# One GpSimd instruction of 1024 columns for each low part of a weight slot

## The reference

```
for layer in range(2):  x = x + mix(rmsnorm(x) @ w_in) @ w_out     # mLSTM, gated linear attention, sparse attention
h = h + 0.5 * swiglu(rmsnorm(h))                                   # FFN 1, inner width 2816
h = h + (gate_a * (attention @ w_a) + gate_g * (gmlp @ w_g)) @ w_out
h = h + 0.5 * swiglu(rmsnorm(h))                                   # FFN 2, inner width 2816
return rmsnorm(h)
```

## Time and profile before

| what | value |
|---|---|
| runs | 1190.82, 1191.22, 1198.76 us |
| profiled execution | 1191.43 us, span in the trace 1189.3 us |
| TensorE (PE) | 1151.8 us busy, 97% |
| VectorE (DVE) | 827.2 us busy, 70%, 1302 instructions |
| ScalarE (ACT) | 652.1 us, 55% |
| GpSimd (POOL) | 735.0 us, 62%, 552 instructions |
| mean granted TensorE clock | 0.991 |
| instructions in the span | 22346 |

### The profile page before, as it was taken

How to read it: one execution, slowest core, us unless ns; L and a number is a source line. 1 busy time by engine, 2 the same in 40 slices (tenths; PEclk the granted TensorE clock), 3 DMA queues, 4 the chain that set the end, 5 groups by cost and what they waited for, 6 DMA issues and landing times.

```text
span 1189.3 us, 22346 instructions
## 1 busy us (share of the span) xinstructions
PE 1151.8 (97%) x8970; PEld 1080.6 (91%) x8970; DVE 827.2 (70%) x1302; ACT 652.1 (55%) x1082; POOL 735.0 (62%) x552
## 2 busy tenths in 40 slices
PE   8979999999997999999999999999999999999996
PEld 6768998999986889899999999999789999999996
DVE  5877777669577876775876666666657667666664
ACT  7655773466575568435746444446566446444443
POOL 5668696567584768945675556566644664645552
PEclk9989999999998999999999999999999999999999
DMA  8443344546543433545466555554534554565550
GB/s 304 161 138 137 125 160 155 171 142 210 181 160 124 150 126 125 184 145 180 139 225 202 201 196 195 195 187 151 206 130 137 182 180 160 177 205 181 183 178 36
DMA packets 64118, 199.84 MB, mean 168 GB/s; under 512 B 6608, under 2 KB 17936, under 8 KB 64016
## 3 DMA queue, kind: packets, MB, share of 16 engines
q1 hardware_dynamic: 60048, 193.74, 47.8%
q10 hardware_dynamic: 3968, 4.69, 1.2%
HBM read 196.57 MB, written 1.84 MB: 167 GB/s over the span
## 4 chain that ended last, share of the span: by engine, by line
PE 85%; DVE 9%; ACT 3%; issue 2%; DMA 1%; ACTq 0%; DVEq 0%
PE ps L1582 47%; PE ps L1633 19%; PE ps L1623 9%; PE ps L1783 2%; DVE xs L930 1%; PE ps L1876 1%; DVE score L1073 1%; PE ps L1592 1%; ACT ring L438 1%; PE ps L1886 1%; DVE gb L1090 1%; DMA par<-in_par 1%; PE ps L1818 1%; PE ps L1857 0%; DVE ring L920 0%
## 5 line engine op out<-in xcount | busy, mean ns | idle before, releaser
L328 POOL TENSOR_TENSOR ring<-raw,ring 128x512 fp32r<-128x512 f32 x498 | 704.2, 1440 | 431.1 <-ACT ring L438 430.5
L1582 PE MATMUL ps<-xs,ring 128*128 128x256 f32 x5040 | 608.5, 281 | 1.9 <-DVE ring L920 1.6
L1582 PEld LDWEIGHTS ps<-xs,ring 128*128 128x128 f32 x5040 | 592.4, 190 | 9.6 <-issue 7.9
L438 ACT ACTIVATE ring<-raw 128x1024 fp32r<-128x1024 f32 x364 | 377.0, 1051 | 111.4 <-PE ps L1633 50.5
L920 DVE TENSOR_TENSOR ring<-raw,ring 128x1024 fp32r<-128x1024 f32 x115 | 162.1, 1411 | 121.9 <-ACT ring L438 121.7
L1633 PE MATMUL ps<-ys,ring 128*128 128x256 f32 x2016 | 241.7, 279 | 1.6 <-DVE ys L982 1.2
L1633 PEld LDWEIGHTS ps<-ys,ring 128*128 128x128 f32 x2016 | 237.2, 189 | 2.5 <-issue 2.5
L1623 PE MATMUL ps<-ring,xs 128*128 128x512 f32 x672 | 165.0, 398 | 0.0
L1623 PEld LDWEIGHTS ps<-ring,xs 128*128 128x128 f32 x672 | 123.0, 188 | 29.0 <-issue 3.6
L757 ACT ACTIVATE ys<-ca 128x256 fp32r<-128x256 f32 x44 | 18.3, 417 | 105.6 <-DVE ca L1377 105.6
L752 ACT ACTIVATE ex<-ex 128x256 f32<-128x256 f32 x44 | 18.2, 418 | 80.8 <-DVE ex L1363 80.8
(11 more groups left out here) (267 smaller groups left out, 1042.2 us busy)
## 6 DMA issues: line engine op xcount, KB each, us to landing
raw<-in_w SPq DMA_DIRECT2D x364, 512.0 KB, 3.5
y<-bias_rows ACTq DMA_DIRECT2D x6, 256.0 KB, 4.5
out_y<-y SPq DMA_DIRECT2D x4, 256.0 KB, 2.5
const<-in_const SPq DMA_DIRECT2D x1, 896.0 KB, 10.5
x<-in_x SPq DMA_DIRECT2D x3, 256.0 KB, 6.6
bias_rows<-lg ACTq DMA_DIRECT2D x1, 768.0 KB, 7.6
dec<-in_wT ACTq DMA_DIRECT2D x1, 512.0 KB, 3.5
qke<-in_ln ACTq DMA_DIRECT2D x1, 512.0 KB, 4.4
```

The lines of the kernel that those rows point to most:

```text
L328: last = pool.tensor_tensor(ring[:, g % RING, 1, half], raw[:, g % RAW, half], ring[:, g % RING, 0, half].bitcast(F32), ALU.subtract)
L438: act.activation(ring[:, g % RING, 0, :], raw[:, g % RAW, :], ACT.Copy).then_inc(S["hi"], 1)
L1582: last = mm(ps[bank][:, half * T:(half + 1) * T], ring[:, slot % RING, wp, (at + k) * P:(at + k + 1) * P], rhs(k, xp), start=(i == 0), sto ...
```

## The change

For each of its 249 slots GpSimd issues one subtraction over all 1024 columns, where it issued two over 512 columns each. The semaphore `lo` is raised by that one instruction; before, it was raised by the second of the two. Nothing else differs.

```
--- before.py
+++ after.py
@@ -323,11 +323,8 @@
                 g = p + RING
                 if not on_vector(p):
                     pool.wait_ge(S["hi"], reg * per + (g + 1))
-                    for a in range(0, SLOT, SLOT // 2):
-                        half = slice(a, a + SLOT // 2)
-                        last = pool.tensor_tensor(ring[:, g % RING, 1, half], raw[:, g % RAW, half],
-                                                  ring[:, g % RING, 0, half].bitcast(F32), ALU.subtract)
-                    last.then_inc(lo[g % RAW], 1)
+                    pool.tensor_tensor(ring[:, g % RING, 1, :], raw[:, g % RAW, :],
+                                       ring[:, g % RING, 0, :].bitcast(F32), ALU.subtract).then_inc(lo[g % RAW], 1)
```

## The result

The changed kernel takes 1238.5 us (median of 4 runs, 1235.9 to 1240.2) against 1195.0 (median of 4, 1190.8 to 1198.8) of the kernel before in the same runs: a ratio of 1.036, 95% interval 1.031 to 1.041. Forecast were 1202 us and a range of 1192 to 1210. The direction was right and so was the mechanism of a single hold (VectorE stands while GpSimd subtracts); the size of the sum was not: about 11 us forecast, 43.5 measured. The profiled execution took 1238.85 us, 47.4 more than that of before.

A forecast was written before the change was run, and what follows sets the result against it. TensorE, busy 97%, was taken to bound the kernel, so only its waits for VectorE count. 2.6 + 3.8 + 3.0 + 1.4 - 0.3 = 10.5 us on 1191.43 gave 1202 us, range 1192 to 1210.

The forecast's parts named there:

- The hold becomes a whole: VectorE instructions behind GpSimd stand for a whole subtraction: a hold of 2.21 us in place of 1.13.
- the signs listed: Expected TensorE waits: L1724 16 us, L1857 4, L2022 near 3, new L1633 near 2 twice; L1582 waits would refute.
- L1724: Long VectorE chain with eight GpSimd slots before this TensorE wait: +1.5 us in each layer, +3.0 in all.
- L1857: VectorE norm chain before this TensorE wait, replayed with four whole subtractions: +1.3 us in each layer, +2.6 in all.
- Start: Very start of the kernel, where slot 2 is just in time: GpSimd's earlier low part allowed a 0.3 us gain.
- FFNs: VectorE's blocked product ends 1.1 us later, still 2.5 in time; with three blocked, 0.2 in time: cost 0.
- the seven places: The places summed, over both layers, each bounded by 0 and one whole hold of 2.2 us: 0 to 15.4.
- Start of the `w_out` part: Three GpSimd slots beside VectorE's norm work delay TensorE's first product there: +1.9 us in each layer, +3.8 in all.
- L2022: Two wholes before VectorE's L1478, where three halves stood, lengthen this TensorE wait: +1.4 us.
- This rival: New waits in the FFNs: VectorE's slack used up, 1222 us, or 1207 to 1212 at a few tiles; chance 0.20.
- absorbed: Rival: VectorE's longer waits fall into free time, so 1191 us, from 1189 to 1195; chance 0.22.
- faster: Rival: GpSimd's lateness limited TensorE through the ring, so 2 us gained, 1189 us; chance 0.03.

The follow-up runs named there:

- e1: The changed kernel with GpSimd's subtraction replaced by 16 memsets of 64 columns, low parts left out of the result: 1168.8 us, 0.987 of the kernel before.
- e14: Kernel before (halves), but whole subtractions for slots GpSimd makes at slots 36 to 46 of each layer: +5.5 and +5.4 us there; total time not given.
- e4: Kernel before (halves), but whole subtractions for the slots of the two FFNs: 1.011 of the kernel before.
- e6: Changed kernel, but halves for slots made before the first layer and up to slot 35 of each layer: 20.9 us under e13.
- e13: The changed kernel run once more, in another group on another chip: 1.043 of the kernel before.
- e15: Kernel before (halves), but whole subtractions for slots made before the first layer and up to slot 35 of each layer: 15 us above the 1203 expected.
- e2: Apparently four subtractions of 256 columns per slot in place of the changed kernel's single one (number not stated in the text): 1178.92 us, 0.9935 of the kernel before.
- e8: A follow-up kernel whose number the text never ties to a change; its change and time cannot be given.

## Why the prediction was wrong

*What bounds the kernel, and GpSimd's own time.* Right. TensorE is held up by its waits for VectorE, no grown wait names GpSimd, and a whole takes 2.35 us against 2.345 estimated.

*The hold becomes a whole.* Right: the excess at the maxima doubled from 1.1 to 2.2 us, and without holds (e1) the kernel is 1.3% faster than before. Of the signs listed, L1721's 15.7 us, L2019's 2.9 and the new waits at L1630 came near; L1854's 8.1 us for 4 and the waits at L1579 in the FFNs, named as a sign of being wrong, did not fit.

*L1724.* The own delay was well sized: L1111, the old L1114, ends at 71.68, 4.95 later, of which 3.6 was there at slot 14: +1.35 against +1.5. Layer 0's stretch lost 3.8 in all, layer 1's 1.5. The rest of layer 0's lies behind the wait, where the clock is granted at 0.50 from 68 to 76 us; before it was 0.53 and 0.61 from 64 to 72. How much of that is the change stays open, since kernels with halves there (e14, e4) showed +2.4 and +1.0 at slot 22.

*L1857.* Here two things failed. The replay is the chain alone, begun at the time and with the lead over TensorE that VectorE had in the trace of before. For the changed kernel the chain itself came out: L905's start to pml's end takes 9.96 us for 8.64, +1.3 as summed, and the L1214 run free. But L905 starts only 1.73 us ahead of the first four L1854 and not 3.66: VectorE had lost 1.9 us of lead to the holds before, and TensorE pays that too. pml comes 3.2 us late, not 1.3, and the clock behind the longer wait adds 2.5 and 1.4 us. The second failure shows in e6 and e14, with their nearly full lead. "Whole 1 runs from 174.65" and "Now no slot is left": the arrivals were those of four L438, but GpSimd at 174.65 was one slot behind. In the trace of before, the slot whose high part ended at 171.88 was begun at 175.64, a lag of 3.8 us; the subtraction I took for the first new arrival was the backlog. So five wholes, not four, lie before pml in e6 and e14, the chain takes 11.96 us (+3.3 for +1.3), and the step is 5.4 to 5.5 us a layer. In the changed kernel this error cost nothing, since VectorE came too late to meet the fifth: that the +1.3 fits there is luck.

*Start.* "I allow a gain of 0.3 us": it lost 3.8 in the first profile and 2.1 in e13 (2.1 to 7.0 in the eight profiles with wholes there, 0.1 at most in e4, e6 and e14, which have halves). L927 is a VectorE chain too, and the replay was not made for it:

```profile
14.05 2.48 POOL L326 TENSOR_TENSOR ring<-raw,ring 128x1024 fp32r<-128x1024 f32 x1
...
16.87 2.50 PE L1589 MATMUL ps<-xs,ring 128*128 128x256 f32 x10 [2.11 <-DVE xs L927]
```

*Places never listed.* The sum took the seven places where TensorE already waited, from the earlier trace rows. Slots 22 to 34 and 112 to 124 were not among them: there TensorE had no wait, but VectorE's chains had slack of less than a hold. One is L1154, one per level, 1.43 and 1.47 us long in two levels of before. Now:

```profile
103.54 2.02 DVE L1151 TENSOR_TENSOR qke<-gq,gs 128x256 f32<-128x256 f32 x1
...
108.59 2.61 DVE L1151 TENSOR_TENSOR qke<-gq,gs 128x256 f32<-128x256 f32 x1
```

TensorE now waits behind it at L1780, 0.5 and 0.6 us in layer 0, and then in the sparse attention, 0.8 us for VectorE's L1203 and 1.2 for ScalarE's L655, whose own delay I did not trace. In all +3.7 and +3.4 us. A third place is slots 34 to 46, +1.9 us a layer: TensorE waits 1.6 us for the convolution L1226, and VectorE comes with less lead to L1854. What lies before slot 36 and the start are the early part, 12.5 us by slot 46 in e15.

*Start of the `w_out` part.* Near: the wait for its first slot grew from 0.2 to 1.5 and 1.6 us, +1.3 and +1.4 for 1.9 each; but "these keep up" did not hold, TensorE also waits 0.6 and 1.6 us for low parts of `ys` there, and the stretches with the gates lost 2.8 and 2.6. *L2022.* The wait grew from 1.4 to 2.9 us, +1.5 for +1.4; the other 2.7 of the stretch lie behind it, at a granted clock of 0.52 from 972 to 976 us and 0.62 to 980: the 16 products of L2019 and the 48 behind them take 2.03 and 7.65 us, before 1.14 and 5.73.

*FFNs.* "2.5 us in time" held for one blocked product; "still 0.2 in time" for three. But L917 and L979, two instructions in a row, each behind a whole, already make TensorE wait 0.4 us, 11 times in the two FFNs, and 2 us at the end of FFN 1. This rival had 0.20 and its price for a few tiles, 5 to 10 us more, was of the size seen in FFN 1 (+9.0); e4, with wholes in the FFNs alone, gives 1.011 (1.007 to 1.014). It should have been in the sum beside the main case and not instead of it. The rivals "absorbed" and "faster" fell.

So of some 37 us missed, about 4 are VectorE's lost lead at L1854 (1.9 in each layer), 7 the clock behind lengthened waits (2.5 and 1.4 measured, 2.7 read at L2019), 7 the level and attention stretches, 4 the start, 8 the FFNs, 4 slots 34 to 46, 2 the `w_out` part and 2 around L1721. What failed is one step in all of them: the sum priced one longer hold at each of seven places where TensorE already waited, each replayed as if all before it had stayed on time, and put the rest of the program and the clock at nothing. Each of my bounds was one hold a place; a place with more instructions in a row can lose several.

## What to carry to other kernels

When a background engine's instruction can block the critical engine, its width is a price paid by the other: look for the width at which the holds are short and the background engine still keeps up (here 256 columns, 0.84 us), and not for the fewest instructions. To price a change of a hold, replay every chain of the blocked engine whose slack is under a few holds, not only those that already make the bottleneck wait, and begin each replay with the backlog of the blocking engine (the lag from its input's end to its own start), not with the arrivals, and with the lead that the blocked engine still has by then. Add to a new stall of TensorE the clock that it costs behind it.

## What the runs showed of the hardware

TensorE's pace in an FFN has two values at one granted clock. In the trace of before, the same 48 products without any wait, once in FFN 1 and once in FFN 2, both at a granted clock of 1.00:

```profile
672.18 5.60 PE L1582 MATMUL ps<-xs,ring 128*128 128x256 f32 x48
...
1111.69 5.82 PE L1582 MATMUL ps<-xs,ring 128*128 128x256 f32 x48
```

Twenty slots take 54.4 or 56.5 us, some 7 us per FFN. It does not follow the width of the subtractions: before had the fast value in FFN 1 and the slow one in FFN 2, e2, e4 and e13 the slow one in FFN 1, e14 and e8 the fast one in both. It fits the spread of the runs of before, 1182 to 1199 us, and it is why the drifts of the experiments are given up to slot 180 only. In the profiles without wholes in an FFN it stays at one value from slot 185 of FFN 1 and slot 302 of FFN 2 on. In the changed kernel's FFNs it goes from one value to the other and back: in FFN 1 the 222nd to the 227th slot of the program take 2.82 to 2.84 us each, the 216th and 217th 2.72.

With wholes an FFN takes about as long at either value. At the slow one they cost nothing: 56.5 us for each 20 slots in FFN 1 of e4 and of e13. At the fast one slots 185 to 245 take 55.1, 57.1 and 56.9 us in the changed kernel, 0.7 to 2.7 us more than 54.4. So the +9.0 and -1.3 us of the table are against a fast FFN 1 and a slow FFN 2 of before; against a fast FFN 2 the second would be some 5 us of loss, an estimate from the 167.8 us that its slots 303 to 362 take and three times 54.4. What sets the value is open.

A `tensor_scalar` that reads one SBUF tensor was blocked too: in the changed kernel L1472 over 512 columns took 0.55 us in one place and 2.63 in the next, where a whole ran from 966.21 to 969.07; at the first GpSimd stood idle from 964.35 to 966.21. The prediction named only instructions with two SBUF inputs.

```profile
964.80 0.55 DVE L1472 TENSOR_SCALAR gv<-gv,rden,rms 128x512 f32<-128x512 f32 x1
...
966.72 2.63 DVE L1472 TENSOR_SCALAR gv<-gv,rden,rms 128x512 f32<-128x512 f32 x1
```

The Trainium skill (SBUF — State Buffer, "Who interferes with whom") counts `tensor_scalar` among the instructions that can take the shared ports; these rows agree.
